# Two transformer blocks on one core: other order at the start, h turned inside the last pieces, keys and values after the convolution's inputs

## The reference

```
block 1, per layer:
  h = x + 0.5 * swiglu(rms(x) ; 1024 -> 2*2816 -> 1024)            # ffn1
  q, k, v, c, g = split(rms(h) @ w_in)                              # mixer 1
  y_attn = window attention(rms(q), rms(k), v, sink, rel_bias) @ w_attn_out
  y_conv = silu(layer_norm(depthwise conv of 31 taps(c_val * sigmoid(c_gate)))) @ w_conv_out
  h = h + (sigmoid(g_attn) * y_attn + sigmoid(g_conv) * y_conv) @ w_o
  h = h + 0.5 * swiglu(rms(h))                                      # ffn2
  x = h + (p @ w_pe_proj) * sigmoid(rms(h) @ w_pe_gate)             # embedding
block 2, per layer:
  x = x + concat(dilated attn, latent attn, differential attn)(rms(x) @ w_in) @ w_o   # mixer 2
  x = x + relu(rms(x) @ w_up)^2 @ w_down                            # ffn
out = rms(x) * final_g
```

## Time and profile before

| | |
|---|---|
| median of 3 runs | 1888.47 us (1888.16 to 1897.19) |
| the profiled execution | 1888.56 us, its span 1886.8 us |
| TensorE matmul | 97% of the span busy |
| VectorE / ScalarE / GpSimd | 59% / 47% / 1% |
| mean granted TensorE clock | 0.988 |
| DMA | 305.27 MB, mean 162 GB/s |

### The profile page before, as it was taken

The page is one execution under the profiler, slowest core; times in us unless marked ns, Lnnn a source line. Parts: engine busy times, 40 slices in busy tenths (PEclk is TensorE's granted clock), DMA queues, the critical chain, the costliest instruction groups (busy, mean ns, idle before and its releaser), DMA issues.

```text
span 1886.8 us, 28888 instructions
## 1 busy us (share of the span) xinstructions
PE 1822.2 (97%) x11400; PEld 1628.6 (86%) x11400; DVE 1114.6 (59%) x1591; ACT 889.2 (47%) x1283; POOL 26.6 (1%) x31
## 2 busy tenths in 40 slices
PE   5999999999999999999999999998999999899997
PEld 4899898789988899888879998787798988779896
DVE  4565477865545555557865554567465556656553
ACT  4343455544434544445554443465453436645351
POOL 0000010000000000001000000000000000000000
PEclk8999999999999999999999999999999999999999
DMA  6465533445555445453345545443255543335551
GB/s 249 169 215 186 182 120 127 149 177 179 179 179 188 170 179 179 168 192 109 134 156 174 185 173 189 154 140 128 91 183 195 179 154 134 112 112 179 181 180 42
DMA packets 45747, 305.27 MB, mean 162 GB/s; under 512 B 5008, under 2 KB 6032, under 8 KB 11824
## 3 DMA queue, kind: packets, MB, share of 16 engines
q1 hardware_dynamic: 45616, 303.43, 45.6%
HBM read 300.26 MB, written 3.15 MB: 161 GB/s over the span
## 4 chain that ended last, share of the span: by engine, by line
PE 81%; issue 12%; DVE 3%; ACT 2%; DMA 1%; DVEq 0%; SPq 0%; POOLq 0%; POOL 0%; ACTq 0%
PE ps L461 13%; PE ps L462 13%; PE ps L463 13%; PE ps L489 11%; PE ps L490 11%; PE ps L491 11%; PE ps L509 1%; PE ps L585 1%; PE ps L769 1%; DVE wlo L1420 1%; PE ps L793 1%; PE ps L595 1%; ACT whi L948 1%; PE ps L617 1%; PE ps L778 0%
## 5 line engine op out<-in xcount | busy, mean ns | idle before, releaser
L1420 DVE TENSOR_TENSOR wlo<-raw,whi 128x2048 fp32r<-128x2048 f32 (+2 forms) x370 | 655.6, 1781 | 495.5 <-ACT whi L948 494.4
L948 ACT ACTIVATE whi<-raw 128x2048 fp32r<-128x2048 f32 (+2 forms) x370 | 551.2, 1502 | 354.5 <-PE ps L463 248.4
L489 PE MATMUL ps<-x_hi,wlo 128*128 128x256 f32 x2048 | 586.0, 286 | 17.8 <-DVE wlo L1420 15.7
L490 PE MATMUL ps<-x_lo,whi 128*128 128x256 f32 x2048 | 582.8, 285 | 0.0
L491 PE MATMUL ps<-x_hi,whi 128*128 128x256 f32 x2048 | 582.5, 284 | 0.0
L489 PEld LDWEIGHTS ps<-x_hi,wlo 128*128 128x128 f32 x2048 | 396.0, 193 | 25.6 <-DVE wlo L1420 17.5
L490 PEld LDWEIGHTS ps<-x_lo,whi 128*128 128x128 f32 x2048 | 396.1, 193 | 0.3
L491 PEld LDWEIGHTS ps<-x_hi,whi 128*128 128x128 f32 x2048 | 396.2, 193 | 0.0
L462 PE MATMUL ps<-wlo,hid_hi 128*128 128x512 f32 x608 | 241.7, 398 | 0.0
L461 PE MATMUL ps<-whi,hid_hi 128*128 128x512 f32 x608 | 239.7, 394 | 0.0
L463 PE MATMUL ps<-whi,hid_lo 128*128 128x512 f32 x608 | 239.5, 394 | 0.0
(11 more groups left out here) (243 smaller groups left out, 1499.3 us busy)
## 6 DMA issues: line engine op xcount, KB each, us to landing
raw<-in_w SPq DMA_DIRECT2D x264, 1024.0 KB, 4.8
raw<-in_w SPq DMA_DIRECT2D x12, 768.0 KB, 4.2
raw<-in_w SPq DMA_DIRECT2D x8, 512.0 KB, 3.3
raw<-in_w SPq DMA_DIRECT2D x4, 576.0 KB, 3.6
line_scratch<-line SPq DMA_DIRECT2D x8, 256.0 KB, 3.2
raw<-in_w SPq DMA_DIRECT2D x2, 864.0 KB, 4.6
bias<-line_scratch SPq DMA_DIRECT2D x1, 1536.0 KB, 9.3
h<-in_x SPq DMA_DIRECT2D x1, 1024.0 KB, 5.3
```

Source lines behind the costliest of these rows:

```text
L489: e.matmul(o, wl, x_hi[:, c, :], start=first and n == 0 and m % 2 == 0, stop=False)
L490: e.matmul(o, wh, x_lo[:, c, :], start=False, stop=False)
L948: e.activation(w_at(whi, j, off, n), raw[:, j % RAW, off:off + n], ACT.Copy).then_inc(s_hi, count)
L1420: e.tensor_tensor(w_at(wlo, j, off, n), raw[:, j % RAW, off:off + n], f32(w_at(whi, j, off, n)), ALU.subtract).then_inc(s_lo, count)
```

## The change

- **Start.** The first 224 columns of the constants come first, then half of x, the two halves of piece 0 as two transfers, the other half of x, pieces 1 to 3, and the rest of the constants and the bias's inputs. ScalarE and VectorE turn two chunks, split half a piece, and so on; the squares of half 0 come after piece 0, those of half 1 after its turn in `ffn1`. A Silu of two elements loads the table first.
- **Bias.** One matmul with `rel_bias` itself as the 8-column stationary operand, at the ninth tick; mask and line have 8 partitions; one DMA broadcasts it.
- **Mixer 1.** c1 goes ahead of kv. Channel 0 is summed on VectorE in two accumulators. Attention's steps wait four instead of one tick between queries and keys.
- **Ends of phases.** Half 0 of the next phase's x is turned inside the last piece: in `mixer1` after chunk 1 of 4, in `embedding` after chunk 2, in `mixer2` before the last chunk, where its low chunks are also kept in other slots of x and the drain comes a piece later. Pieces behind `w_pe_gate` and `w_pe_proj` are `halved`.
- **End.** h times the gain is made as soon as h is known, and the last scale is shared by VectorE and ScalarE.

```
@@ plan
-                out += [piece("w_in", l, LO + HI, (512, 768))] + c1
+                out += c1 + [piece("w_in", l, LO + HI, (512, 768))]
@@
-MIXERS = ("w_in", "w_attn_out", "w_conv_out", "w_o", "w_in_2", ...
+MIXERS = ("w_in", "w_attn_out", "w_conv_out", "w_o", "w_pe_gate", "w_pe_proj", "w_in_2", ...
-    return j > AHEAD and ORDER[j - AHEAD][0] in MIXERS and len(ORDER[j][2]) % 2 == 0
+    return j < 2 or j > AHEAD and ORDER[j - AHEAD][0] in MIXERS and len(ORDER[j][2]) % 2 == 0
@@ tensor: bias_of_heads
+                for _ in range(8):
+                    yield
+                b = spare("line")
+                e.wait_ge(s_rb, 48)
+                e.matmul(TB[b][0:8, :], T1["rb"][:, :], T1["oh"][:, :], start=True, stop=True).then_inc(s_tp, 1)
@@ tensor: mixer1 (scalar and vector alike)
-                simple(kv_, X, need, bank("mix", l, 2), True, True)
+                columns_(c1[0], bank("mix", l, 2), "mix", l)
+                columns_(c1[1], bank("mix", l, 2), "mix", l)
                 bg.append(att)
+                simple(kv_, X, need, bank("mix", l, 3), True, True)
...
-                simple(b[1], X, need, b1, False, True)
-                x_of_h(*nxt, 0)
+                simple(b[1], X, need, b1, False, True, mid=lambda: x_of_h(*nxt, 0))
@@ tensor: embedding
+                simple(b[1], X, need, b1, False, True, mid=lambda: x_of_h(*nxt, 0), mid_at=2)
@@ tensor: mixer2, the tail
-                drain(gen)
...
                 out_of(a[1], bks[10], MB[0:2], False)
+                drain(gen)
                 out_of(b[1], bks[11], MB[0:2], False)
...
-                out_of(b[1], bks[11], MB[2:4], True)
+                out_of(b[1], bks[11], MB[2:3], False)
                 x_of_h(*nxt, 0)
+                out_of(b[1], bks[11], MB[3:4], True)
@@ scalar and vector: use
                 for i in range(n):
                     if i % 2 == 1 and i < n - 1:
                         tick(steps)
-                        if mid is not None:
-                            mid()
+                    if mid is not None and i == mid_at:
+                        mid()
+                    if i % 2 == 1 and i < n - 1:
                         high(NUM[spec] + AHEAD)
@@ scalar: ffn1, first phase
+                    x_of_h(f, l, 1)
+                    norm_sums(f, l, 1)
+                    high(2)
+                    spread(f, l)
+                    high(NUM[u[1][0]] + AHEAD)
@@ scalar: the tail of mixer2
                 high(NUM[a[1]] + AHEAD)
+                drain(gen)
                 x_of_mix(l, 2, 1)
-                use(a[1])
+                x_of_h(*nxt, 0)
                 norm_sums(*nxt, 0)
-                use(b[1])
-                x_of_h(*nxt, 0)
+                high(NUM[b[1]] + AHEAD)
                 norm_sums(*nxt, 1)
@@ scalar: the start
+            e.activation(sm2[:, 120:122], mh[:, 0:2], ACT.Silu)
             e.wait_ge(s_cst, 16)
+            x_pair("ffn1", 0, 0)
+            high(0, True)
+            x_pair("ffn1", 0, 2)
+            high(0)
             norm_sums("ffn1", 0, 0)
-            x_of_h("ffn1", 0, 0)
-            norm_sums("ffn1", 0, 1)
+            high(1)
@@ vector: conv_taps, channel 0
+                for tap in range(TAPS):
+                    p = tap % 2
+                    own[p] = step(tap_of(0, tap, acc[:, 2 * p, :], own[p], None if p else k("conv_b", 4 * l)))
...
+                e.tensor_tensor(acc[:, 0, :], acc[:, 0, :], acc[:, 2, :], ALU.add).then_inc(s_acc, 1)
@@ vector: the tail of mixer2
+                low(NUM[a[1]] + AHEAD, True)
+                drain(gen)
                 low(NUM[a[1]] + AHEAD)
                 x_of_mix(2, 1)
-                use(a[1])
                 residual(a[1], bank("mix2", l, 10), lambda t: 1.0, *nxt, 0)
-                use(b[1])
                 x_of_h(*nxt, 0)
+                low(NUM[b[1]] + AHEAD)
                 residual(b[1], bank("mix2", l, 11), lambda t: 1.0, *nxt, 1)
@@ the end
+            e.tensor_scalar(h[:, 0, :], fin[:, 0, :], rsq(12, 4), None, ALU.mult, ALU.bypass).then_inc(s_fin, 1)   # vector
+            e.activation(h[:, 1, :], fin[:, 1, :], ACT.Copy, scale=rsq(12, 5)).then_inc(s_fina, 1)                 # scalar
```

More of the change, by code:

```diff
@@ L445, in spare_frees, with rows @@
                 f[i] = list(when)
-            def rows(spec, jobs, need, mid=None, done=True, steps=1):
+            def rows(spec, jobs, need, mid=None, mid_at=1, done=True, steps=1):
                 j = NUM[spec]
@@ L467, in rows, with simple @@
                         tick(steps)
-                        if mid is not None:
-                            mid()
+                    if mid is not None and n == mid_at:
+                        mid()
                 tick(steps)
-            def simple(spec, op, need, bk, first, last, base=0, mid=None, steps=1):
+            def simple(spec, op, need, bk, first, last, base=0, mid=None, mid_at=1, steps=1):
                 w, n = width(spec), len(spec[2])
-                rows(spec, [(i * w, w, op, c - base, bk, first and i == 0, last and i == n - 1) for i, c in enumerate(spec[2])], need, mid, steps=steps)
+                rows(spec, [(i * w, w, op, c - base, bk, first and i == 0, last and i == n - 1) for i, c in enumerate(spec[2])], need, mid, mid_at, steps=steps)
             def columns_(spec, bk, name, l):
@@ L540, in bias_of_heads @@
             def bias_of_heads():
[L541 to L547, removed]
+                for _ in range(8):
                     yield
+                b = spare("line")
+                e.wait_ge(s_rb, 48)
+                e.matmul(TB[b][0:8, :], T1["rb"][:, :], T1["oh"][:, :], start=True, stop=True).then_inc(s_tp, 1)
+                spare_frees(b, (s_lw, 1))
             def ffn1(l, f, nxt):
@@ L633, in attention1 @@
                     spare_frees(b, (s_qT, 3 * l + n + 1))
-                yield
+                for _ in range(4):
+                    yield
                 b = spare(("kT", l))
@@ L949, in high, with use @@
                     split[0] += 1
-            def use(spec, ticks=None, mid=None, end=True, steps=1):
+            def use(spec, ticks=None, mid=None, mid_at=1, end=True, steps=1):
                 high(NUM[spec] + AHEAD, True)
@@ L1136, in mixer1 @@
                 tick()
+                use(c1[0])
+                use(c1[1], end=False)
+                sigmoid_of(1)
+                tick()
+                bg.append(att)
                 use(kv_, end=False)
@@ L1177, in mixer1 @@
                 norm_sums(*nxt, 0)
[L1178 to L1179 removed]
+                use(b[1], mid=lambda: x_of_h(*nxt, 0))
                 norm_sums(*nxt, 1)
@@ L1421, in low, with use @@
                     split[0] += 1
-            def use(spec, ticks=None, mid=None, steps=1):
+            def use(spec, ticks=None, mid=None, mid_at=1, steps=1):
                 low(NUM[spec] + AHEAD, True)
@@ L1522, in hid @@
                     e.tensor_tensor(lo, pr, f32(hi), ALU.subtract).then_inc(s_hlo, 1)
-                use(u[0][0])
-                x_of_h(f, l, 1)
-                use(u[1][0])
-                spread(f, l)
+                if F == 0:
+                    tick()
+                    tick()
+                    x_of_h(f, l, 1)
+                    norm_done(f, l)
+                    low(2)
+                    spread(f, l)
+                    low(NUM[u[1][0]] + AHEAD)
+                    tick()
+                    tick()
+                else:
+                    use(u[0][0])
+                    x_of_h(f, l, 1)
+                    use(u[1][0])
+                    spread(f, l)
                 for j in range(11):
@@ new lines, in tap_of @@
+                def tap_of(ch, tap, a, own, bias):
+                    x, w = pad[:, ch, tap:tap + 256], k("conv_w", (l * 4 + ch) * 31 + tap)
+                    if own is None:
+                        e.wait_ge(s_pad0, 2 * l + 2)
+                        e.wait_ge(s_pad, 2 * l + ch // 2 + 1)
+                        if bias is None:
+                            return e.tensor_scalar(a, x, w, None, ALU.mult, ALU.bypass)
+                        return e.tensor_scalar(a, x, w, bias, ALU.mult, ALU.add)
+                    e.wait_ge(s_dv, own)
+                    return e.scalar_tensor_tensor(out=a, in0=x, scalar=w, in1=a, op0=ALU.mult, op1=ALU.add)
@@ new lines, in conv_taps @@
+                while 2 * l + 2 > pads[0]:
+                    yield
+                own = [None, None]
+                e.wait_ge(s_acc, 3 * l + 1)
+                for tap in range(TAPS):
+                    for p in range(2):
+                        i = tap_of(2 + p, tap, acc[:, 2 + p, :], own[p], k("conv_b", 4 * l + 2 + p))
+                        if tap < TAPS - 1:
+                            own[p] = step(i)
+                        else:
+                            i.then_inc(s_acc, 1)
+                        count += 1
+                        if count % 4 == 0:
+                            yield
@@ L1612, in attention1 @@
```

(5 more changed lines are left out.)

249 lines of the change are left out of this document (122 added, 127 removed).

## The result

The changed kernel takes 1869.69 us (median of four, 1867.87 to 1871.65) against 1888.37 beside it: a ratio of 0.989 (95% interval 0.988 to 0.991). It is faster by 18.7 us where 45 were forecast, and its time lies outside the forecast's range. The profiled execution took 1869.03 us with a span of 1867.2.

The account below looks back on a forecast made before the run. TensorE was taken to bound the kernel, its matmuls filling 1822.2 of 1886.8 us. Savings of 25.6 + 10.3 + 2.1 + 1.7 + 4.8 + 0.6 = 45.1 us from 1888.5 gave 1843.4, range 1834 to 1856.

Parts of the forecast that it names:

- the ends of the phases: Holes after first mixers, embeddings and second mixers shrink or go by earlier turns and halved pieces: 2.1, 1.7 and 4.8 us.
- the bias's work: At the start, the 4.9 us `rbw` hole goes and fewer bias matmuls save 9.6 us.
- the mixer's end: End of each first-block mixer: the reorder shortens TensorE's stop ahead of the norm's turns; 10.3 us over both layers.
- part 1: The kernel's start: earlier first matmul, bias work removed, less low clock; 25.6 us saved, bounds 17 to 29.
- one stays: At the start, eight bias matmuls cost 10.9 us and one of them remains: 9.6 us saved.
- part 2: End of each first-block mixer: the reorder gains 10.3 us, after 0.3 per layer for late keys; bounds 0 to 12.
- line 638 waiting: Sign against the forecast: TensorE waiting at this line in the first mixers would make it wrong.
- Line 509: Sign against the forecast: a wait at this line in the first mixers would make it wrong.
- The start: First transfers cut and reordered, bias work removed, less low clock: first weight matmul at about 8.95, 25.6 us saved.
- the halving's 1.7: After each embedding, halved pieces let VectorE subtract sooner; the hole shrinks from 2.6 to 1.8, 1.7 us for two.
- rival (c): Low-clock stretches inside the later mixers vanish as their place moves: up to 7 us more won, 1837; chance 0.14.
- The kernel's end: Last scale shared by VectorE and ScalarE after the last matmul: 0.6 us saved, bounds -0.5 and 1.2.

Follow-up runs that it names:

- the kernel with both mended: Changed kernel with the store from 128 partitions and VectorE's keys work put ahead of the taps: 1842.37 us, ratio 0.975 to the kernel before.
- the better version: Changed kernel with the 128-partition store, keys ahead of taps, and ScalarE's earlier split of the next phase's piece in the embeddings: 1839.03 us, ratio 0.9735 to the kernel before.

## Why the prediction was wrong

The sum missed by 26.3 us. The runs give 22.1 us to one term and 5.2 to another, and the kernel with both mended takes 1842.4 where 1843.4 was forecast. That it comes within 1 us is partly luck: in their own runs the ends of the phases and the bias's work are worth more than forecast and the mixer's end less.

1. **The step that failed is part 1's "one stays".** It counted the bias's matmuls and the widened columns, and nothing for the store that now goes out as one transfer from eight partitions. Its DMA cost was not bounded, though the trace before had eight stores of 256 KB from 128 partitions, landing in 3.2 us each (median):
```profile
line_scratch<-line SPq DMA_DIRECT2D x8, 256.0 KB, 3.2
```
   No row of the profile before has a store from so few partitions, and there the forecast owed both ends: eight times the store's 3.2 us is 25.6 us at the old rate, and sixteen times that if the rate went by partitions. Even the lower end is longer than the 20.6 us that five pieces take beside it. The store ran at 50 GB/s for 44.5 us in front of the weight pieces, and that cost 19.2 us of hole and 2.3 of clock. No rival held it either: none has a transfer in it beyond the first 25 us.
2. **The keys, part 2.** "5.7 us for copies ... I make that 5.5, and take 0.3 per layer off": measured 3.2 per layer. The chain itself was right (subtract and four taps in it), but I started it at the keys' landing; VectorE was two ticks of taps (2.85 us and more) behind. The prediction named line 638 waiting as what would make it wrong, and that line (642 now) waited. Line 509 (513 now), the other one named, waited a little longer than before too: 0.6 in each first mixer against 0.2.
3. **The start held.** x half landed at 5.6 (4.6 forecast), first weight matmul 9.99 (8.95), `dg` hole 1.39 (2.0), piece 5 begun at 45.36 (44) in place of 70.2. So up to there the start gave 24.8 us of its 25.6, and what failed came behind it. One us late throughout, since x's first landing took 4.4 us and not 3.4.
4. **The mixer's end held** at 8.9 against 10.3 once the keys are out of it.
5. **The ends of the phases** were undersized: 12.5 against 6.9 (8.6 without the halving's 1.7, which stays in that run). The holes are 7.9 of it; 3.1 is busy time, that is clock, and the rest lies between the profiled run and the median. First mixers 2.1 and second mixers' 5.1 came; the embeddings' came from the halving as forecast (1.8 each forecast, 1.74 measured).
6. **The clock.** Three kernels that differ in the store alone (128 partitions, eight apart, sixteen) show 1802.6, 1804.7 and 1804.8 us of TensorE's busy time, and the four runs of the better version lie at 1837.7 twice, 1840.3 and 1840.8. So rival (c)'s difference is real in kind and a few us in size. The holes that (c) compares were 3.6 and 2.5 us long; the changed kernel has a closer pair, the keys' holes of 3.21 and 3.20 us. The windows behind them:
```profile
291.73:296.00 4.27, 4.27 (x13) 3.41 (x14) 3.71 (x6) 2.70 (x3) 0.00 (x0) 0.60 0.47 155
880.54:890.00 9.46, 9.46 (x40) 6.92 (x41) 8.20 (x20) 4.94 (x9) 0.00 (x0) 1.00 0.32 111
```
   Behind the first the clock fell, behind the second it stayed.

The kernel's end: 8.9 us from the last matmul instead of 9.6, so 0.7 saved where 0.6 was forecast. The forecast's own terms there (2.48 less 1.1 and 0.4) add up to 1.0.

## What to carry to other kernels

Before work is taken from the busy engine, price the transfer that replaces it by where its data lie: partitions, how close together, and what stands behind it in its queue. The slow transfer cost nothing here once nothing was queued behind it and nobody waited for it in order; either of the two alone still made a hole. Pieces beside it were slowed too, and here they had been issued early enough for that. An engine that is 60% busy can still make a chain late: read where in its order the chain's first step stands, not when its input is there.

## What the hardware showed

- A 2 MB store from eight neighbouring partitions ran at 50 GB/s (44.5 us), from sixteen neighbours at 98 (23.2 us), from eight that lie four apart at 205 (done within 12.7 us), and from 128 at 385 (8.1 us).
- Weight pieces on the other queue passed the slow store but were slowed by it: 19.2 us to landing in one run, a median of 12.3 in another, against 31.7 behind it in the same queue and 4.8 undisturbed.
- The DMA share was 0.45 at 50 GB/s, 0.53 at 205, 0.91 at 98 and 1.01 at 385: a share can stand high while little gets through, and only the GB/s beside it tell.
- Behind two holes of 3.2 us in one execution the clock fell once (0.60 over 4.27 us) and once stayed at 1.00.
